# Second attention of a two-block kernel: permuted q, k columns, a rope swap on VectorE, and the first v transposes behind the lead steps

## What is computed

```
# first attention ("fox", 16 heads of 64): causal, with a bias from a cumulative sum of gates
q, k, v, f = split(x @ a_w_in);  c = cumsum(log_sigmoid(f + b_f))
o = softmax(q k^T / 8 + c_i - c_j) v
# second attention ("diff", 8 units of 2 maps of 64): k, v from kv_w, q from w_q
q1, q2, k1, k2 = rope(...)       # halves of 32: [t1*cos - t2*sin, t2*cos + t1*sin]
a = softmax(q1 k1^T / 8) - lam * softmax(q2 k2^T / 8)      # masked by chunks of 64 keys
o = rmsnorm(a v) * g * (1 - lambda_init)
```

## Time and profile before

| | us |
|---|---|
| median of 3 runs (lowest, highest) | 2008.67 (2006.48, 2010.9) |
| the profiled execution, its own time | 2004.82 |
| its span, first to last instruction | 2003.0 |
| PE busy in the span | 1851.6 (92%) |
| POOL busy | 1060.2 (53%) |
| DVE busy | 829.6 (41%) |
| ACT busy | 810.5 (40%) |
| mean granted TensorE clock, share of full | 0.967 |

### The profile page before, as it was taken

One profiled execution on the slowest core, in us unless ns is written; L12 is line 12 of the kernel. 1 busy time (PEld: TensorE's weight loads), 2 busy tenths in 40 slices (PEclk: granted clock), 3 DMA queues, 4 the chain that ended last, 5 costly groups with the idle time before them and its releaser, 6 DMA issues.

```text
span 2003.0 us, 27255 instructions
## 1 busy us (share of the span) xinstructions
PE 1851.6 (92%) x8879; PEld 1534.8 (77%) x8879; DVE 829.6 (41%) x1383; ACT 810.5 (40%) x1698; POOL 1060.2 (53%) x937
## 2 busy tenths in 40 slices
PE   6687999999998999899999999788888999999997
PEld 5466888888886788788888888676766788888887
DVE  6996300001134555574333222445555653333224
ACT  4313422332233544445444422545655364444223
POOL 6776655556562222256666655534444566666551
PEclk9797999999998999999999999998989999999998
DMA  4212233333324444223333233213232223333331
GB/s 127 64 32 64 73 96 95 94 100 93 93 62 106 111 109 117 76 82 95 94 97 98 87 101 92 66 48 74 52 73 63 85 62 96 94 94 90 99 91 67
DMA packets 330002, 170.87 MB, mean 85 GB/s; under 512 B 46978, under 2 KB 320468, under 8 KB 329940
## 3 DMA queue, kind: packets, MB, share of 16 engines
q1 hardware_dynamic: 328594, 169.49, 30.5%
q10 hardware_dynamic: 1346, 0.59, 0.1%
HBM read 151.10 MB, written 2.10 MB: 76 GB/s over the span
## 4 chain that ended last, share of the span: by engine, by line
PE 74%; DVE 10%; ACT 5%; issue 5%; POOL 2%; DMA 1%; SPq 1%; ACTq 0%; DVEq 0%; POOLq 0%
PE bank L828 21%; PE bank L829 21%; PE bank L830 21%; DVE xin L1840 2%; DVE work L1840 2%; PE attended L830 2%; PE attended L829 2%; PE attended L828 2%; DVE xres L1778 1%; ACT pmap L1488 1%; PE turned L1140 1%; ACT attended L1643 1%; DVE small L1941 1%; ACT XH L1347 1%; ACT WH L1297 1%
## 5 line engine op out<-in xcount | busy, mean ns | idle before, releaser
L656 POOL TENSOR_TENSOR WL<-raw,WH 128x512 fp32r<-128x512 f32 (+3 forms) x656 | 791.2, 1228 | 671.3 <-ACT WH L1297 670.3
L828 PE MATMUL bank<-XL,WH 128*128 128x512 f32 x1456 | 589.2, 405 | 55.5 <-POOL WL L656 26.4
L830 PE MATMUL bank<-XH,WL 128*128 128x512 f32 x1456 | 573.6, 394 | 0.0
L829 PE MATMUL bank<-XH,WH 128*128 128x512 f32 x1456 | 573.6, 394 | 0.0
L1297 ACT ACTIVATE WH<-raw 128x512 fp32r<-128x512 f32 (+3 forms) x656 | 338.3, 566 | 356.1 <-PE bank L830 208.8
L828 PEld LDWEIGHTS bank<-XL,WH 128*128 128x128 f32 x1456 | 279.0, 192 | 114.5 <-POOL WL L656 35.7
L830 PEld LDWEIGHTS bank<-XH,WL 128*128 128x128 f32 x1456 | 278.4, 191 | 59.8
L829 PEld LDWEIGHTS bank<-XH,WH 128*128 128x128 f32 x1456 | 279.7, 192 | 51.7
L830 PE MATMUL bank<-HH,WL 128*128 128x512 f32 (+1 forms) x528 | 201.1, 381 | 0.0
L829 PE MATMUL bank<-HH,WH 128*128 128x512 f32 (+1 forms) x528 | 201.1, 381 | 0.0
L828 PE MATMUL bank<-HL,WH 128*128 128x512 f32 (+1 forms) x528 | 201.0, 381 | 0.0
(11 more groups left out here) (271 smaller groups left out, 2703.2 us busy)
## 6 DMA issues: line engine op xcount, KB each, us to landing
raw<-in_ffn_w_in SPq DMA_DIRECT2D x88, 512.0 KB, 3.8
raw<-in_w_gate SPq DMA_DIRECT2D x22, 512.0 KB, 3.9
raw<-in_w_up SPq DMA_DIRECT2D x22, 512.0 KB, 3.9
raw<-in_ffn_w_out SPq DMA_DIRECT2D x28, 384.0 KB, 3.3
raw<-in_ffn_w_out SPq DMA_DIRECT2D x28, 320.0 KB, 3.2
raw<-in_a_w_in SPq DMA_DIRECT2D x16, 512.0 KB, 4.1
raw<-in_kv_w SPq DMA_DIRECT2D x32, 256.0 KB, 3.0
raw<-in_w_in SPq DMA_DIRECT2D x12, 512.0 KB, 3.8
```

The costliest lines, as they stand in the source:

```text
L656: pool.tensor_tensor(WL[:, s, ks, :], raw[:, g.slot(RAW), ks, :], WH[:, s, ks, :].bitcast(F32), ALU.subtract).then_inc(w_lo, 1)
L828: pe.matmul(out_, wh, xl, start=start, stop=False)
L829: pe.matmul(out_, wh, xh, start=False, stop=False)
L830: return pe.matmul(out_, wl, xh, start=False, stop=stop)
```

## The change

The columns of a q or k item are written to `WH` and `WL` in another order: before (map, half, 32), after (half, map, 32), so that rows 0 to 63 of the projected tile hold both maps' first halves. Each split instruction of such an item now covers one half of the columns and all eight row tiles, in place of all columns and four row tiles (`turned`), and PE waits for both before the first step. The last two items of the stage, which belong to the output product, keep their order. The four ACT copies are gone; DVE does the cos product and two products of 64 rows, each reading one half of the bank and writing to the other 64 rows of `rot_sin`. `pad_q` needs eight DMAs of 32 rows, and the sine table comes by four DMAs, signs in the new order. The slots of the splits, of the rope instructions, of the norm of the unit before (one slot or two earlier) and of `value_out` (ahead of `osb`) move; steps move to later slots. In both attentions the first unit's `turn_v` comes behind the eight lead steps, and unit 0's splits and gates come in another order; in the first, SP issues the load of unit 1's q item ahead of `pack_q(0)` and that of its k item ahead of `pack_k(0)`.

```diff
-DIFF_STEPS = (2, 2, 2, 2, 2, 2, 2, 3, 2, 2, 3, 0)
-FIRST_DIFF_STEPS = (0, 0, 1, 2, 2, 2, 2, 2, 1, 1, 3, 0)
+DIFF_STEPS = (1, 1, 2, 2, 2, 2, 2, 3, 2, 3, 4, 0)
+FIRST_DIFF_STEPS = (0, 0, 0, 2, 2, 2, 2, 2, 1, 2, 3, 0)
+        def half_of_maps(x, h):
+            return x.rearrange("p k (m h c) -> p k m h c", m=2, h=2)[:, :, :, h, :]
+        def maps_of_half(x, h):
+            return x.rearrange("p k (h m c) -> p k h m c", h=2, m=2)[:, :, h, :, :]
...
@@ SP, first attention
+                if n == 4 or n == 5:
+                    fox_load(1, j)
                 if 0 <= u < UNITS and j == 0:
                     pack_q(u)
...
@@ SP, pad_q
-                        r = slice(HEAD * c, HEAD * c + HEAD)
-                        sp.dma_start(z[r, c, :].bitcast(F32), x[r, slot, 0, :].bitcast(F32)).then_inc(q_padded, 16)
+                        for r in rows_of_map(c):
+                            sp.dma_start(z[r, c, :].bitcast(F32), x[r, slot, 0, :].bitcast(F32)).then_inc(q_padded, 16)
...
@@ POOL, unit_lows, units with an attended unit
+                if iu is not None:
+                    next_low(iu, 0)
+                if not first_unit(au):
+                    sub_low(au + -1)
+                if iu is not None:
+                    next_low(iu, 1)
+                    rope_sum(iu, 0)
+                    rope_low(iu, 0)
+                    next_low(iu, 2)
+                    rope_sum(iu, 1)
+                    rope_low(iu, 1)
+                    next_low(iu, 3)
...
@@ PE
-                    pe.wait_ge(w_lo, g.times(2).n(1))
-                if k == kt - kt // 2:
+                    pe.wait_ge(w_lo, g.times(2).n(2 if turned else 1))
+                if k == kt - kt // 2 and not turned:
                     pe.wait_ge(w_lo, g.times(2).n(2))
...
-                    turn_v("qkv1", au)
-                    weave(unit_steps("qkv1", iu), fox_slot(au), FIRST_FOX_STEPS, DT)
+                    weave(unit_steps("qkv1", iu), fox_slot(au), FIRST_FOX_STEPS, DT, lambda: turn_v("qkv1", au))
...
-                    turn_v("qkv2", au)
-                    weave(unit_steps("qkv2", iu), diff_slot(au), FIRST_DIFF_STEPS, DT)
+                    weave(unit_steps("qkv2", iu), diff_slot(au), FIRST_DIFF_STEPS, DT, lambda: turn_v("qkv2", au))
...
@@ ACT, first attention, unit 0
+                        if au is None:
+                            if j == 2:
+                                head_gates()
+                            if j < 3:
+                                unit_high("qkv1", iu, j + 1)
...
@@ ACT, load_rope
-                act.dma_start(rope[:, :, :], A["rope"].rearrange("a p s -> p a s")).then_inc(rope_in, 16)
+                act.dma_start(rope[:, 0, :], A["rope"][0]).then_inc(rope_in, 16)
+                for b in range(4):
+                    r = 0 if b >= 2 else 32
+                    act.dma_start(rope[32 * b:32 * b + 32, 1, :], A["rope"][1][r:r + 32, :]).then_inc(rope_in, 16)
...
@@ ACT, second attention
-                            for r in range(4):
-                                o = r + 1 - 2 * (r % 2)
-                                act.activation(rot[32 * r:32 * r + 32, :], bank[j][32 * o:32 * o + 32, :], ACT.Copy).then_inc(rot_ready, 1)
...
+            HIGH_AT = (3, 5, 8, 11)
...
+                    if iu is not None:
+                        if sl in HIGH_AT:
+                            unit_high("qkv2", iu, HIGH_AT.index(sl))
+                        if sl in (6, 10):
+                            rope_hi(iu, (sl - 6) // 4)
+                    if sl == 12:
+                        if iu is not None:
+                            value_out("qkv2", iu)
+                        act.wait_ge(o_done[0], au.n(UNITS + 1))
...
@@ DVE
+            def rope_products(iu, j):
+                scale = 1.0 if j else HEAD ** -0.5
+                dve.wait_ge(item_done, iu.times(4, STAGES["qkv2"][0] + j + 1).n())
+                dve.wait_ge(qk_lo, iu.times(2, j).n() + OPEN)
+                own.did(dve.scalar_tensor_tensor(out=qk[:, :], in0=bank[j][:, :], scalar=scale, in1=rope[:, 0, :],
+                                                 op0=ALU.mult, op1=ALU.mult))
+                for h in range(2):
+                    of, to = slice(HEAD * h, HEAD * h + HEAD), slice(HEAD - HEAD * h, P - HEAD * h)
+                    if h:
+                        own.sync()
+                    ins = dve.scalar_tensor_tensor(out=rot_sin[to, :], in0=bank[j][of, :], scalar=scale, in1=rope[of, 1, :],
+                                                   op0=ALU.mult, op1=ALU.mult)
```

More of the change, by code:

```diff
@@ L447, in at, with last_unit, weave_units @@
             return bass.ds(u.n(), 1)
-        def weave_units(Fori, part):
+        def last_unit(u):
+            return isinstance(u.it, int) and u.base == UNITS - 1
+        def weave_units(Fori, part, apart=0):
             part(Nth(0), None)
             part(Nth(1), Nth(0))
-            with Fori(0, (UNITS - 2) // 2) as it:
+            with Fori(0, (UNITS - 2) // 2 - apart) as it:
                 for j in range(2):
                     part(Nth(2 + j, it, 2), Nth(1 + j, it, 2))
+            for u in range(UNITS - 2 * apart, UNITS):
+                part(Nth(u), Nth(u - 1))
             part(None, Nth(UNITS - 1))
@@ L1604, in sub_high, with rope_hi @@
                 act.activation(OH[:, at(u), :], osb[:, :].rearrange("p (a s) -> p a s", a=1), ACT.Copy).then_inc(sub_hi, 1)
+            def rope_hi(iu, j):
+                act.wait_ge(roped, iu.times(2, j + 1).n())
+                act.activation(QKH[:, iu.slot(2), j, :], qk[:, :], ACT.Copy).then_inc(qk_hi, 1)
+            HIGH_AT = (3, 5, 8, 11)
             def diff_part(iu, au):
                 first = 4 * UNITS
[L1608 removed]
@@ new lines, in diff_part @@
+                for sl in range(13):
+                    if sl == 2:
+                        value_hi(1, au)
+                        if before is not None:
+                            sub_root(before)
+                    if sl in (4, 6, 8, 10):
+                        i = sl // 2 - 2
+                        map_hi(i % 2, au.times(2, first + i // 2), 0, i)
+                    if sl < 8:
+                        exps(sl, au.times(4, first + sl // 2))
+                    if sl == 4 and before is not None:
+                        sub_high(before)
+                    if iu is not None:
[5 more added lines that the diff above has]
+                        if iu is not None:
+                            value_out("qkv2", iu)
+                        act.wait_ge(o_done[0], au.n(UNITS + 1))
+                        act.wait_ge(sub_lo, au.n() + OPEN)
+                        act.activation(osb[:, :], ob[0][:, :], ACT.Copy).then_inc(o_read[0], 1)
+                        act.wait_ge(o_read[0], au.n(UNITS + 1) + OPEN)
+                        act.activation(osq[:, :], osb[:, :], ACT.Square).then_inc(sub_sq, 1)
```

210 lines of the change are left out of this document (92 added, 118 removed).

## The result

The changed kernel takes 1946.5 us (median of 4 runs, 1944.7 to 1950.4), the kernel before 2008.1 us beside it: ratio 0.9695, 95% interval 0.9675 to 0.9715, that is 61.5 us less by the medians. The profiled execution took 1947.9 us, its span is 1946.1 us in place of 2003.0, and PE is busy 95% of it.

What follows compares the result with a forecast made beforehand. PE, bound by waits and the clock loss behind them: -38.7 (six periods) - 7.7 - 5.6 - 8.5 (starts, first period) + 2.5 (table) = -58.0 us, from median 2008.7 to 1950.7, said as 1950; range 1938 to 1976.

Steps and rivals of the forecast that it cites:

- The first period: Second attention, first unit: 28.6 us before, 23.0 us predicted with the long gap gone, -5.6 us.
- the table: Norm ahead of the second attention: four more DMAs on ACT's queue, +2.5 us, bounds 0 and 2.5.
- the two starts: Lead steps directly behind v: second attention's score 0 -7.7 us; first attention's -8.5 us, bounds -5 and -9.
- the six periods: Second attention, steady units: period falls from 32.95 to 26.5 us, -38.7 us over six.
- gap of 0.8 us: Steady unit's end: wait left from k's low part and SP's DMAs together, 0.8 us, without clock loss.
- v split sooner ... The 3.7 us and the 2.3 us of clock go: Second attention, steady units: v's `high` moves from slot 8 to 5, ending the 3.7 us `WL` wait and 2.3 us clock loss.
- the k chain: Score 7 to next score 0: k's products, sum, rounding and rest take 13.4 us against PE's 11.8; gap 0 to 1.6.
- Rope: Second attention: ACT loses 4.7 us a unit; DVE's two 64-row products for one of 128 add 1.3 us a unit.
- The collision: Steady units: POOL's sum blocks DVE's combination of the third map; gap 1.6 us, 33.9 us gained in place of 38.7.
- the SP chain: Unit's end: eight `pad_q` DMAs, k item's load and copy, then `value_out`, 10.4 us against about 10.5; 0 to 0.8 us.
- Strided splits: Second attention's q and k splits with runs of 32 elements: no change taken; bounds the same and twice the time.
- Slower: Rival, chance 0.04: strided passes cost many times plain ones; at six times, period 39.6 us, whole +23 us, 2032.

Runs made afterwards that it cites:

- three parts back: Changed kernel with the second attention's old step counts, ScalarE's four rope copies per tile and v's late split put back: 1970.6 us (0.9815).

## Why the prediction was right, and where its reasons were not

**The total** was right: -56.8 us by marks against -58.0, and the median of 1946.5 against 1950. Some of this is luck. The first period (+2.0 us) and the table (+0.9) came out worse than said, the two starts and the six periods better (-0.7, -0.8, -0.8). The six periods were worked out as a unit without waits (25.7 us; 25.53 with `value_out` moved) and a gap of 0.8 us, and such a sum comes out whichever edit takes the waits away.

**The step "v split sooner ... The 3.7 us and the 2.3 us of clock go" was wrong in its cause.** The waits and the clock loss did go, but they go without it: put back late in the changed kernel it costs 0.1 us a unit. The early split does take the wait for `WL` away by itself, as the prediction said (the run with the old counts and the copies), and with the copies on ACT it shortened the first period by some 3 us; in the steady units the time came back elsewhere and the period grew by 1.0 us. The prediction read rightly that ACT reached `WH` only behind the four copies, but not what held the copies: not k's last step but the exponential of score 7, behind DVE operations held up beside POOL. Taking the copies away, which it booked as ACT being emptier and as +1.3 us on DVE, is worth 2.3 us a unit, and the two steps moved behind score 7, which it used only in the sum for the k chain, are worth 1.8. The other half of the 6.6 us a unit lies in the new order of the work on the engines and the columns; its cause is argued above from the trace and stays open. A wait that is removed in a loop hands over to the chain next in line; that chain had been counted (13.4 us against 11.8 us), but for the changed kernel, not for each part.

**Rope.** Right: 0.69 us for 64 rows, written across the halves, so +1.4 us a unit where I took +1.3. DVE is nevertheless less busy than before, since operations that had been drawn out beside POOL are shorter: the 1.63 us of the last combination are 0.75 us now, and L2060's 1.42 us (384 columns) are 0.42 us.

**The collision.** DVE's L2107, a product of one column with both inputs in SBUF, takes 0.16 us alone and 0.73 us where it starts at 1413.06 within POOL's sum (1412.47 to 1413.77):

```profile
1413.06 0.73 DVE L2107 TENSOR_TENSOR small<-small 128x1 f32<-128x1 f32 x1
...
1412.47 1.30 POOL L822 TENSOR_TENSOR work<-work 128x512 f32<-128x512 f32 x1
```

It ends when the sum does. The rope products, which read PSUM, ran at 0.68 us beside POOL (L2087 at 1409.92). The Trainium skill, page "SBUF — State Buffer", section "SBUF: two separate sides", has DVE's operations on two SBUF inputs and GpSimd's that read SBUF exclude each other; the trace agrees with the rule: L2107 ends 0.02 us from the end of the sum. But it costs 0.57 us on a chain with 0.87 us to spare, so the 1.6 us gap that the prediction worked out from it did not come. In the kernel before such collisions cost more, as shown above.

**The gap of 0.8 us** was 0.6, on the SP chain that the prediction had as 0 to 0.8; the k chain gave none. **Strided splits** cost nothing, as taken. **The starts**: -8.5 and -9.2 us against -7.7 and -8.5; the run with transposes first shows 5.3 us for the order of work alone.

**The first period** was mis-sized: 23.0 us predicted, 25.0 and 26.8 in the two profiles of the same kernel. The matmuls did not run at full clock as the sum had it: the granted clock was 0.93, and there were 1.4 us of wait for a combined map (DVE's L2109, ahead of the transposes at 1313.62).

**The table** was mis-sized at its bound: +3.4 us where 2.5 was the highest. The four issues took less than said (1.87 us, 0.47 each, where 2.5 was taken); what was left out is that a wait of 1.6 us became one of 3.4 us and the clock fell behind it. The prediction had the rule from its own row 3 and used it in the steady units alone.

**A slip in a rival.** "Slower" takes the net gain of the starts as 16.8 us; its terms (7.7, 5.6 and 8.5 less 2.5) give 19.3, which moves its threshold from 35.8 to 36.2 us and touches nothing else.

## What to carry to other kernels

Before crediting a wait's end to the edit that moves the late operation, ask what stood ahead of it and whether another edit in the same change takes that away; put back each part alone and in pairs, since here the obvious part was worth nothing in the steady units. In a loop bound by waits, price each added microsecond of idling with the clock behind it: 1.3 us more of waiting a unit cost 1.8 us. The issues of small transfers belong on a queue whose engine is not in the middle of a chain of norms.

## What the runs showed of the hardware that I had not expected

A wait of the same length does not always cost the clock. With the copies on ScalarE PE waits 1.6 us ahead of score 0 in every unit; the periods are 29.45, 27.71, 27.80, 29.55, 27.84 and 29.90 us. In the unit from 1403.41 the score matmuls right behind the wait still run at full clock, and the half-speed stretch (0.63 us for 512 columns in place of 0.39) follows from 1404.9 to some 1409 us, for the loss of 1.8 us. Waits of 0.6 us alone never did this (granted clock 1.00 over six periods). With waits of 1.8 us and 0.9 us in every unit all six periods are long, 30.6 to 31.0 us. Waits of 2.4 us with three parts back gave 0.94 in three units and 1.00 in the other three. In the kernel before the clock fell behind each wait of 3.5 us, but in two of six units the matmul right behind it still took 0.50 us (at 1429.20), and 0.63 us was seen only from 1430.85 on.

A VectorE operation of a single column can take 0.73 us or 1.17 us in place of 0.16 us when it starts beside a POOL operation on SBUF, and ends when that one does (L2107 at 1413.06, L2059 at 1419.74); its length then says nothing of its own work. L2060, with one tensor as input, was drawn out likewise, 1.42 us in place of 0.42.
